# Attention sweep: values of three key tiles at a time, GpSimd adding the exponentials in trios

## What is computed

```python
keys = jnp.concatenate([_apply_rope(ak, cos, sin), cache['k'].astype(ak.dtype)], axis=1)
vals = jnp.concatenate([av, cache['v'].astype(av.dtype)], axis=1)
y_at = _block_attention(_apply_rope(aq, cos, sin), keys, vals)
...
def one(qblk):
    s = jnp.einsum('bqkgd,bskd->bkgqs', qblk, k).astype(jnp.float32) * scale
    p = jax.nn.softmax(s, axis=-1).astype(v.dtype)
    return jnp.einsum('bkgqs,bskd->bqkgd', p, v)
```

## Time and profile before

| | us |
|---|---|
| median of 3 runs (lowest, highest) | 2375.9 (2374.77, 2378.68) |
| the profiled execution | 2374.82 |
| its span | 2373.0 |
| the sweep, from the first score matmul to the end of its last ones pass | 1161.81 to 1396.15, 234.3 |
| PE busy in the span | 2295.2 |
| DVE, ACT, POOL busy in the span | 1426.0, 805.5, 224.7 |

### The profile page before, as it was taken

One profiled execution on the slowest core, in us unless ns is written; L12 is line 12 of the kernel. 1 busy time (PEld: TensorE's weight loads), 2 busy tenths in 40 slices (PEclk: granted clock), 3 DMA queues, 4 the chain that ended last, 5 costly groups with the idle time before them and its releaser, 6 DMA issues. The chain is left out here.

```text
span 2373.0 us, 43700 instructions
## 1 busy us (share of the span) xinstructions
PE 2295.2 (97%) x17959; PEld 2029.6 (86%) x17959; DVE 1426.0 (60%) x2212; ACT 805.5 (34%) x1398; POOL 224.7 (9%) x245
## 2 busy tenths in 40 slices
PE   6999999999999899998899999998999999999997
PEld 5887779999999889998655569877999999998886
DVE  5331266533555467665677646768676676677877
ACT  5321132213333233223344444325223222234444
POOL 0000000001110011112222101000111121120001
PEclk9999999999999999999999999999999999999999
DMA  6324632235452532214101138421222222259434
GB/s 279 120 85 182 225 112 107 100 135 202 155 173 86 198 107 87 83 66 158 44 19 48 56 112 312 154 92 59 79 104 91 76 107 91 73 183 271 129 98 124
DMA packets 126877, 295.60 MB, mean 125 GB/s; under 512 B 19808, under 2 KB 63280, under 8 KB 117376
## 3 DMA queue, kind: packets, MB, share of 16 engines
q1 hardware_dynamic: 98112, 238.67, 29.9%
q10 hardware_dynamic: 24640, 39.46, 4.5%
q0 software_dynamic: 3968, 15.21, 1.7%
HBM read 207.83 MB, written 85.53 MB: 124 GB/s over the span
## 5 line engine op out<-in xcount | busy, mean ns | idle before, releaser
L62 PE MATMUL ps<-prj_w,h_hi 128*128 128x512 f32 (+1 forms) x864 | 254.2, 378 | 4.2 <-DVE h_lo L755 4.2
L62 PE MATMUL ps<-h_hi,fill_whi 128*128 128x384 f32 x672 | 235.8, 351 | 4.7 <-ACT fill_st L1119 2.4
L62 PE MATMUL ps<-h_lo,fill_whi 128*128 128x384 f32 x672 | 226.6, 337 | 3.5 <-issue 3.5
L62 PE MATMUL ps<-wt 128*128 128x320 f32 (+2 forms) x1046 | 227.2, 327 | 2.3 <-DVE merged L3308 1.3
L62 PE MATMUL ps<-h_hi,fill_wlo 128*128 128x384 f32 x672 | 226.5, 337 | 0.0
L62 PE MATMUL ps<-ys,mergedr 128*128 128x256 f32 (+1 forms) x1056 | 219.9, 297 | 0.4 <-issue 0.4
L62 PE MATMUL ps<-zb,mergedr 128*128 128x320 f32 (+2 forms) x764 | 199.8, 326 | 4.9 <-issue 2.7
L62 PE MATMUL ps<-zb,wt 128*128 128x384 f32 (+3 forms) x758 | 200.2, 325 | 0.0
L62 PEld LDWEIGHTS ps<-prj_w,h_hi 128*128 128x128 f32 x864 | 157.3, 190 | 43.0 <-issue 10.6
L62 PEld LDWEIGHTS ps<-wt 128*128 128x128 f32 x1046 | 179.6, 189 | 16.6 <-issue 2.6
L62 PEld LDWEIGHTS ps<-ys,mergedr 128*128 128x128 f32 x1056 | 174.6, 191 | 0.7 <-issue 0.7
(11 more groups left out here) (512 smaller groups left out, 4654.1 us busy)
## 6 DMA issues: line engine op xcount, KB each, us to landing
wraw<-in_w_ffn_in SPq DMA_DIRECT2D x22, 1024.0 KB, 5.1
prj_raw<-in_w_ada SPq DMA_DIRECT2D x16, 1024.0 KB, 5.9
fill_raw<-in_w_fill SPq DMA_DIRECT2D x30, 512.0 KB, 4.4
wtf<-a_dram SPq DMA_DIRECT2D x55, 256.0 KB, 2.7
bg_dram<-fill_st ACTq DMA_DIRECT2D x72, 192.0 KB, 2.0
xf<-bg_dram POOLq DMA_DIRECT2D x24, 576.0 KB, 7.4
tok_dram<-prj_tst ACTq DMA_DIRECT2D x45, 256.0 KB, 2.1
prj_raw<-in_w_tok SPq DMA_DIRECT2D x10, 1024.0 KB, 7.3
```

Of the source, the lines that this page charges most:

```text
L62: mm = pe.matmul(out, lhs[a], rhs[b], start=first and n == 0, stop=last and n == 2, skip_group_check=onto)
```

## The change

The sweep keeps its scores, shift scores and their number, and regroups the rest:

- `pt` has six buffers and not five; the two `pair` buffers go, and DVE's three additions per tile with them.
- PE multiplies values in three visits per tile: three slots' values together in slots 3, 6 and 8.
- POOL adds each trio of exponentials in place, two additions of 128x1024 (`add_trio`), once the values of the trio are done. One ones pass per trio is made over that sum: in slots 6 and 8 and, for the last trio, in slot 3 of the next tile. The last trio of the last tile is passed singly, without POOL.
- ACT's exponentials wait for POOL's first addition, second addition and the ones pass of the trio two before, by buffer.
- POOL's rotation is cut in halves that stand between the additions; it reads the rotation table itself, so that DVE's copy of it (L2433) goes.
- On DVE the reciprocal stands behind head 2 and the product with the reciprocals behind head 5; the norm of a query tile starts one tile earlier, and both splits stand at the tile's end, with `norm_b` behind them. In the last tile `ahead` stands before the product.
- On SP the load of the next queries is issued before the wait for the finished rows.

```diff
-    RING = 5
-    PAIRS = 3
-    PAIR_DONE, P_DONE = (1, 2, 4), (3, 5, 6)
-    PAIR_AT = (4, 6, 8)
+    RING, TRIO = 6, 3
+    LASTG = (LAT // P) * NT // TRIO - 1
...
-            pair = [over(f"pair{i}", [P, KV, G * P]) for i in range(2)]
...
-            gp.wait_ge(sem["qd"], 3)
-            gp.tensor_tensor(qrs[:], qms[:], khalf[:, 0:AH], ALU.pow).then_inc(sem["qpow"], 1)
-            def rope(n):
-                gp.wait_ge(sem["qd"], 4 * n + 4 + 3)
+            def inverse_norm(n):
+                gp.wait_ge(sem["qd"], 4 * n + 3)
                 gp.tensor_tensor(qrs[:], qms[:], khalf[:, 0:AH], ALU.pow).then_inc(sem["qpow"], 1)
+            def rope(n, e):
                 gp.wait_ge(sem["qd"], 4 * n + 4 + 4)
                 x = qn[:].rearrange("p h (d e) -> p h d e", e=2)
                 o = qr[:].rearrange("p h (d e) -> p h d e", e=2)
-                w = lambda c: qtb[:, c, :].unsqueeze(1).broadcast_to([P, AH, HD // 2])
+                w = lambda c: qtab[:, n, c, :].unsqueeze(1).broadcast_to([P, AH, HD // 2])
+                a, b = (0, 1) if e == 0 else (2, 3)
+                gp.tensor_tensor(u1[:], x[:, :, :, 0], w(a), ALU.mult).then_inc(sem["rope"], 1)
+                gp.tensor_tensor(u2[:], x[:, :, :, 1], w(b), ALU.mult).then_inc(sem["rope"], 1)
+                gp.wait_ge(sem["rope"], 6 * n + 3 * e + 2)
+                gp.tensor_tensor(o[:, :, :, e], u1[:], u2[:], ALU.subtract if e == 0 else ALU.add).then_inc(sem["rope"], 1)
+                gp.wait_ge(sem["rope"], 6 * n + 3 * e + 3)
+            def add_trio(n):
+                a, b, c = (pt[(TRIO * n + x) % RING] for x in range(TRIO))
+                gp.wait_ge(sem["pv"], n + 1)
+                gp.tensor_tensor(c[:], c[:], a[:], ALU.add).then_inc(sem["paired"], 1)
+                gp.wait_ge(sem["paired"], 2 * n + 1)
+                gp.tensor_tensor(c[:], c[:], b[:], ALU.add).then_inc(sem["paired"], 1)
+            inverse_norm(0)
+            for n in range(2):
+                inverse_norm(n + 1)
                 for e in range(2):
-                    a, b = (0, 1) if e == 0 else (2, 3)
-                    gp.tensor_tensor(u1[:], x[:, :, :, 0], w(a), ALU.mult).then_inc(sem["rope"], 1)
-                    gp.tensor_tensor(u2[:], x[:, :, :, 1], w(b), ALU.mult).then_inc(sem["rope"], 1)
-                    gp.wait_ge(sem["rope"], 6 * n + 3 * e + 2)
-                    gp.tensor_tensor(o[:, :, :, e], u1[:], u2[:], ALU.subtract if e == 0 else ALU.add).then_inc(sem["rope"], 1)
-                    gp.wait_ge(sem["rope"], 6 * n + 3 * e + 3)
-            for n in range(LAST + 1):
-                rope(n)
+                    rope(n, e)
+            inverse_norm(3)
+            for i in range(LAST + 1):
+                if i:
+                    add_trio(3 * i - 1)
+                if i + 2 <= LAST:
+                    rope(i + 2, 0)
+                add_trio(3 * i)
+                if i + 2 <= LAST:
+                    rope(i + 2, 1)
+                add_trio(3 * i + 1)
+                if i + 3 <= LAST:
+                    inverse_norm(i + 4)
...
-                if kv == 0 and i >= 2:
+                if kv == 1 and i >= 2:
...
-            def values(i, j):
-                n = NT * i + j
-                pe.wait_ge(sem["ex"], 2 * n + 2)
-                if j == 0:
+            def values(i, g):
+                if g == 0:
                     if i:
                         pe.wait_ge(sem["evict"], i)
                     else:
                         pe.wait_ge(sem["b0ev"], 24)
-                for kv in range(KV):
-                    mm = pe.matmul(ps[kv * HD:kv * HD + HD, OB, :], va[:, j, kv, 0:HD], pt[n % RING][:, kv, :],
-                                   start=j == 0, stop=j == NT - 1)
+                for j in range(TRIO * g, TRIO * g + TRIO):
+                    n = NT * i + j
+                    pe.wait_ge(sem["ex"], 2 * n + 2)
+                    for kv in range(KV):
+                        mm = pe.matmul(ps[kv * HD:kv * HD + HD, OB, :], va[:, j, kv, 0:HD], pt[n % RING][:, kv, :],
+                                       start=j == 0, stop=j == NT - 1)
                 mm.then_inc(sem["pv"], 1)
...
+            def sums(n):
+                i, g = divmod(n, NT // TRIO)
+                if g == 0 and i:
+                    pe.wait_ge(sem["rc"], i)
+                if n < LASTG:
+                    pe.wait_ge(sem["paired"], 2 * n + 2)
+                    mm = add(pt[(TRIO * n + TRIO - 1) % RING], g == 0, g == 2)
+                else:
+                    for x in range(TRIO):
+                        mm = add(pt[(TRIO * n + x) % RING], False, x == TRIO - 1)
                 mm.then_inc(sem["sums"], 1)
-            def pair_sums(i, p):
-                u = PAIRS * i + p
-                pe.wait_ge(sem["paired"], u + 1)
-                if p == 0 and i:
-                    pe.wait_ge(sem["rc"], i)
-                add(pair[u % 2], p == 0, False)
-            def sums(i, j):
-                add(pt[(NT * i + j) % RING], False, j == NT - 1)
...
-                    if i and j == 2:
-                        spread_sums(i - 1)
+                    if more and j >= 1:
+                        shift_scores(i + 1, j - 1)
                     if more and j == 5:
                         shifts(i + 1, 0)
-                    if more and 1 <= j < NT - 1:
-                        shift_scores(i + 1, j - 1)
-                    if j:
-                        values(i, j - 1)
-                    if j in PAIR_AT:
-                        pair_sums(i, PAIR_AT.index(j))
-                    if j >= 7:
-                        sums(i, j - 1)
-                    if more and j == NT - 2:
-                        shift_scores(i + 1, AH - 1)
+                    if j == 3:
+                        if i:
+                            sums(3 * i - 1)
+                        values(i, 0)
+                    if j == 6:
+                        if i:
+                            spread_sums(i - 1)
+                        values(i, 1)
+                        sums(3 * i)
+                    if j == 8:
+                        values(i, 2)
+                        sums(3 * i + 1)
                 if more:
                     shifts(i + 1, 1)
-                values(i, NT - 1)
-                sums(i, NT - 1)
+                else:
+                    sums(LASTG)
...
-                if n >= RING:
-                    o, oj = divmod(n - RING, NT)
-                    act.wait_ge(sem["pv"], n - RING + 1)
-                    if oj < 2 * PAIRS:
-                        act.wait_ge(sem["paired"], PAIRS * o + oj // 2 + 1)
-                    else:
-                        act.wait_ge(sem["sums"], (NT - PAIRS) * o + P_DONE[oj - 2 * PAIRS])
+                b, r = divmod(n - RING, TRIO)
+                if b >= 0 and r < 2:
+                    act.wait_ge(sem["paired"], 2 * b + r + 1)
+                if b >= 0 and r == 2:
+                    act.wait_ge(sem["sums"], b + 1)
                 for kv in range(KV):
                     act.wait_ge(sem["s2"], 2 * n + kv + 1)
                     act.activation(pt[n % RING][:, kv, :], ps[:, ST + kv, :], ACT.Exp, scale=QS).then_inc(sem["ex"], 1)
...
-            def norm_b(n, table):
+            def norm_b(n):
                 v.wait_ge(sem["qpow"], n + 1)
-                if table is not None:
-                    v.tensor_copy(qtb[:], table)
                 v.tensor_tensor(qn[:], q[:], wide(qrs[:], AH), ALU.mult).then_inc(sem["qd"], 1)
...
-            def pair_up(i, p):
-                u = PAIRS * i + p
-                v.wait_ge(sem["ex"], 2 * (NT * i + 2 * p + 2))
-                if u >= 2:
-                    o, op = divmod(u - 2, PAIRS)
-                    v.wait_ge(sem["sums"], (NT - PAIRS) * o + PAIR_DONE[op])
-                a, b = ((NT * i + 2 * p + x) % RING for x in range(2))
-                v.tensor_tensor(pair[u % 2][:], pt[a][:], pt[b][:], ALU.add).then_inc(sem["paired"], 1)
             def tile(i):
-                if i >= 1:
-                    inverted(i - 1)
+                if i == -1:
+                    norm_a(3)
+                if 0 <= i < NT - 3:
+                    norm_b(i + 3)
                 for h in range(AH):
                     if i < LAST:
                         shift(i + 1, h)
-                    if i >= 1 and h == 0:
+                    if i >= 1 and h == 2:
+                        inverted(i - 1)
+                    if i == LAST and h == 5:
+                        ahead()
+                    if i >= 1 and h == 5:
                         normed(i - 1)
-                    if i >= 0 and h in (1, 3, 5):
-                        pair_up(i, h // 2)
-                    if 0 <= i < NT - 3 and h == 2:
-                        norm_a(i + 3)
-                    if 0 <= i < NT - 3 and h == 3:
-                        norm_b(i + 3, qtab[:, i + 2])
-                    if 0 <= i + 2 <= LAST and h == 5:
-                        next_split(i + 2, 0)
```

(15 more changed lines are left out.)

12 lines of the change are left out of this document (5 added, 7 removed).

## The result

| | kernel before | changed kernel |
|---|---|---|
| median (lowest to highest, runs) | 2375.05 us (2373.34 to 2379.4, 8) | 2385.86 us (2383.17 to 2391.42, 8) |
| profiled execution: time, span | 2374.8, 2373.0 us | 2383.17, 2381.4 us |
| ratio of the times | | 1.0044, 95% interval 1.0033 to 1.0056 |

The changed kernel is slower, by 10.8 us between the medians (7.8 to 13.3 by the interval). The forecast was 2389.

What follows compares the result with a forecast made beforehand. PE, busy 97% of the span, was taken as the bound. Six middle tiles add 8.1 us, tile 0 saves 0.9, the opening 0.75, the last tile adds 6.9: 13.3 more, 2389 us, range 2377 to 2402.

Steps and rivals of the forecast that it cites:

- PE's own work: Middle tile: PE's work without the new waits falls by 3.7 us to 26.55.
- chain of maxima: Middle tile: shift scores wait for DVE's maximum, 0.67 us at four steps and 0.2 at one, 2.9 in all.
- copy of the queries (qm), ACT: Middle tile: scores of group 1 wait 0.35 us for ACT's copy; copies between ACT's exponentials add 0.1.
- split held by POOL: Middle tile's start: POOL's additions hold DVE's cast and subtraction, so PE waits 1.7 us at the second query turn.
- PE's loss: Middle tile: values save 0.9 us, ones passes 1.5, score groups 0.45, other boundaries 0.5, the old wait 0.35.
- rival E: Middle tiles: the chain of maxima doesn't bind, tiles take 27.0 us, total 2356; chance 0.07.
- POOL against DVE: Tile's end: POOL's 2.4 us additions and DVE's two-input operations exclude each other, the cast held too; tile becomes 31.6.
- B: Split: the cast isn't held by POOL's addition; a tile takes 30.5 us, total 2383; chance 0.20.
- C: POOL and DVE get by each other; tiles 29.9 us, last tile +3.4, total 2376; chance 0.13.
- Tile 0 and opening: Tile 0 takes 28.5 us against 29.36; the opening loses a split amid the heads, 0.75 us less.
- The last tile: Ends at 30.7 us, 6.9 more, on a ones pass waiting for POOL's additions; PE's own queue alone gives 3.4 more.
- rival D: POOL's additions take 2.9 us, or PE's clock falls after longer waits; total 2399; chance 0.18.

Runs made afterwards that it cites:

- e1: Changed kernel, but DVE's maximum reads one of its three banks of shift scores (384 of 1152 columns); 2357.76 us.
- e2: Changed kernel, but POOL's additions touch 8 of 1024 columns, all waits and the order kept; 2373.09 us.
- e3: Changed kernel, but up to tile 5 POOL starts the last trio's additions only after DVE's splits and norm; 2380.88 us.
- e8: Changed kernel with three added 128x384 matmuls behind the scores of six slots of the last tile; 2384.47 us.
- e7: Changed kernel with value products issued one key tile per slot in the last tile alone; 2381.51 us.
- e9: Changed kernel, but the last tile's middle trio goes through the ones pass tile by tile, without POOL's addition; 2388.28 us.
- e4: Changed kernel with value products again one key tile per slot, POOL's trio sums and three ones passes kept; 2380.78 us.
- e5: e4 with the norm of the queries one head earlier in DVE's order; 2361.64 us, ratio 0.9946 to the kernel before.

## Why the prediction was right, point by point

In the middle tiles the forecast and the measured time rest on the same mechanisms, with most terms within half a microsecond. The opening and the last tile came out right in size for other reasons than mine; that the sum is this close owes something to luck. Per middle tile, from start to start of the rows of tile 2:

| term | forecast | measured |
|---|---|---|
| visit of three key tiles | 2.73 | 2.72 (1227.12 to 1229.84) |
| PE's own work | 26.55 | 26.7 (27.65 between the waits, less 6 times 0.16 for running out); 26.0 in e1 |
| chain of maxima | 2.9 | 2.7 (four waits of 0.51, 0.50, 0.58, 0.47, and 4 times 0.16); 3.4 by e1 |
| copy of the queries (qm), ACT | 0.45 | 0.46 (0.30 and 0.16) |
| split held by POOL | 1.7 | 1.42 (1.27 and 0.15); 1.5 by e2 and e3 |
| tile | 31.6 | 31.28 |

- **PE's loss.** Right. Values fell by 0.97 for 0.9 and the ones passes by 1.65 for 1.5; in e1, where the maxima don't interfere, the 36 score passes of a tile take 9.4 us instead of 9.5, of it 0.3 of running out ahead of the two waits left: 0.4 saved for 0.45.
- **Chain of maxima.** Right in size, and in four of five places (the wait of 0.2 between slots 5 and 6 isn't there): 14.6 us of waits in 28 places and 28 times 0.16 make 19, for 20 forecast. I had put the wait at 0.67 as one number; it is 0.5 of waiting and 0.16 of running out, which the busy time hides. e1 shows that it is DVE's maximum, and rival E falls. Its 3.4 are more than the rows' 2.7, since the shift scores behind a wait also take longer (5.07 us for the eight of a tile, 4.58 in e1): the border between the chain and PE's own work isn't sharp, their sum of 29.4 is.
- **POOL against DVE.** Right. Each addition takes 2.36 to 2.37 undisturbed for 2.4 taken, and the cast is held (1.34), which decides against B: its tile would have been 30.5. C falls with it, its 29.9 being what e2 and e3 give without the meeting. The Trainium skill (SBUF — State Buffer, Who interferes with whom) has a DVE operation with two SBUF inputs and a GpSimd one that reads SBUF exclude each other, and says that a cast can contend too; the rows above agree, with 2.54 for 0.43 and 1.34 for 0.29. The Trainium skill (GPSIMD Engine Reference, Elementwise) has 4497 ns for an addition of 2048 columns. Half of that, an estimate of 2.25 for 1024, is 0.1 under the rows.
- **Tile 0 and opening.** Tile 0 took 28.48 for 28.5. The opening's 0.7 for 0.75 is luck. The wait that I had in mind went whole, 1.2 and not 0.75, as the other kernels with this opening show; in the profiled pair the clock hid it and gave 0.6 elsewhere.
- **The last tile** was right in size (31.29 for 30.7) and its working was wrong. The step that failed is "the ones pass of slots 3 to 5 also needs both POOL additions ... 28.8. The tile ends at 30.7". POOL's sum was there just in time, at 1402.38, 29.35 after the tile's start, since PE itself came to that pass at 1402.44. I had PE at 10.4, 14.75, 20.0 and 25.4 after the tile's start behind the first visit, the scores of slot 6, the second visit with its ones pass, and the last visit; it was there at 12.8, 18.3, 24.0 and 29.4. What held PE was the clock, after slots with score products alone that wait for ACT. I had named a fall of the clock only in rival D, as something dearer. With the clock held up, by 3.7 us of added matmuls (e8), the step comes out as I had it: the sum ends at 28.4 after the start for 28.8, the tile at 30.3 for 30.7. Two causes of nearly the same size stood in parallel, and I had one of them: the size was luck.
- **Sum.** 13.3 forecast; the sweep gave 13.2 and the opening -0.7, so 12.5. Less the 4.3 of the stages ahead, that is the 8.4 between the two profiled executions, but for 0.2. The medians differ by 10.8, with 7.8 to 13.3 in the interval: the forecast's 13.3 stands at the upper end of that.

What stays open is when the clock begins to fall. With work in the gaps (e8) and with the values spread (e7) it stayed at 1.00, in one trace each; with the same gaps it fell behind the first wait of 0.8 (changed kernel), the second (e9) or neither (e2), and no run varied the gaps.

## What to carry to other kernels

Merging small groups of one engine's work saves their boundaries, but each group also covered a hand-over between other engines; before merging, write down for every chain (here shift scores, maximum, shift scores: 2.24 us) what of the engine's work is left inside one period. Work put on GpSimd is free here only where no VectorE instruction on the path meets it: place both engines' orders together, since moving one collision can make another (e4); where the ones on the path pass each other, as in e5's middle tiles, PE waits for none of them. And a stage should be asked for its second limit: the removed one may lie only a microsecond over the next (e8).

## What the runs showed of the hardware

- Beside an addition of GpSimd (128x1024, 2.37 us) not only two-input operations of VectorE are held, but a cast of 128x256 with one input (1.34 for 0.29) and a scaling of 128x8 (1.50 for 0.17). Both end right behind the addition (0.15 and 0.04). GpSimd loses as well when VectorE's operations are long: its addition takes 2.6 and 3.4 us beside VectorE's 128x1152 subtractions, and 3.3 (changed kernel) and 4.3 (e8) beside those of 128x2048.
- TensorE's granted clock went to the 1.2 GHz level after a wait of 2.29 us in a tile that was otherwise full (e4), though not after each such wait (tile 2 stayed at 1.00), and in the last tile of the changed kernel, right behind waits of 0.81 and 1.56 us. With 0.5 to 0.7 us of matmuls added in six slots it stayed at 1.00 there, even behind a wait of 1.54 (e8). The point of the fall isn't the same in every execution: e2 kept 1.00 behind two waits of 0.80.
- The last pass before a wait takes 0.40 us from its start to the begin of the wait where 0.24 is usual, so 28 waits of 0.5 cost 4.5 us beyond what the list of waits adds up to.
